# Mixer stage of a hybrid attention step on Trainium2: the order of VectorE's queue, three kinds of steps moved to GpSimd, and four buffers for the output weights

## What is computed

```
og  = rmsnorm(o_fwd + o_bwd, gla_norm) * silu(gg)            # gated linear attention, 8 heads of 64
s   = concat([q k_local * scale + mask, q k_context * scale, sink])
p   = softmax(s)[..., :-1]                                    # windowed attention, one sink logit per head
osw = p v
xs  = xs + g1 * (concat([og, osw]) @ w_o)
```

## Time and profile before

| | us |
|---|---|
| median of 3 runs (range) | 1693.15 (1691.63 to 1693.45) |
| the profiled execution, its own time | 1686.72 |
| its span | 1684.9 |
| slot 0 begins (first L1846) | 415.17 |
| slots 35, 46 begin | 605.74, 660.68 |
| the turn after the slots (L2187) | 699.05 |

### The profile page before, as it was taken

The page is one execution under the profiler, slowest core; times in us unless marked ns, Lnnn a source line. Parts: engine busy times, 40 slices in busy tenths (PEclk is TensorE's granted clock), DMA queues, the critical chain, the costliest instruction groups (busy, mean ns, idle before and its releaser), DMA issues. The chain is left out here.

```text
span 1684.9 us, 31914 instructions
## 1 busy us (share of the span) xinstructions
PE 1597.7 (95%) x11618; PEld 1396.7 (83%) x11618; DVE 1009.1 (60%) x1563; ACT 682.9 (41%) x1205; POOL 993.5 (59%) x738
## 2 busy tenths in 40 slices
PE   4999999998899987899999999999999999999997
PEld 1998778997778765688888999989978899998996
DVE  2733565666675565455876566665695545545468
ACT  2514224224454545312354444444535444444441
POOL 1711554655564865002487777777898667677672
PEclk7999999999999989999999999999999999999999
DMA  9354665659555554233662322313235132231322
GB/s 325 98 157 135 198 206 177 224 178 264 166 171 170 164 158 126 107 125 126 212 224 64 100 65 85 100 50 100 87 104 175 61 100 67 83 100 50 100 64 100
DMA packets 211450, 225.93 MB, mean 134 GB/s; under 512 B 52752, under 2 KB 171664, under 8 KB 208144
## 3 DMA queue, kind: packets, MB, share of 16 engines
q1 hardware_dynamic: 209248, 224.46, 41.8%
q10 hardware_dynamic: 2096, 0.02, 0.1%
HBM read 177.22 MB, written 47.24 MB: 133 GB/s over the span
## 5 line engine op out<-in xcount | busy, mean ns | idle before, releaser
L3127 PE MATMUL ff_banks<-h_xop,h_whi 128*128 128x320 f32 x888 | 275.2, 310 | 5.9 <-DVE wo_raw L2931 3.1
L3129 PE MATMUL ff_banks<-h_xop,h_whi 128*128 128x320 f32 x888 | 274.4, 309 | 0.0
L3128 PE MATMUL ff_banks<-h_xop,h_whi 128*128 128x320 f32 x888 | 274.3, 309 | 0.0
L2951 DVE TENSOR_TENSOR ff_acc<-ff_acc,ff_banks 128x512 f32<-128x512 f32 x294 | 199.3, 681 | 99.0 <-PE ff_banks L3156 98.9
L3154 PE MATMUL ff_banks<-h_wlo 128*128 128x512 f32 x600 | 234.3, 390 | 1.6 <-DVE ff_acc L2951 0.7
L3156 PE MATMUL ff_banks<-h_wlo 128*128 128x512 f32 x600 | 233.4, 389 | 0.0
L2793 POOL TENSOR_TENSOR h_whi<-mid_raw,h_whi 128x512 fp32r<-128x512 f32 x149 | 207.3, 1407 | 1.4 <-ACT h_whi L2645 1.4
L2805 POOL TENSOR_TENSOR h_wlo<-mid_raw,h_wlo 128x320 fp32r<-128x320 f32 x128 | 116.6, 912 | 129.4 <-ACT mid_raw L2682 129.4
L3127 PEld LDWEIGHTS ff_banks<-h_xop,h_whi 128*128 128x128 f32 x888 | 166.7, 188 | 9.5 <-issue 5.3
L3128 PEld LDWEIGHTS ff_banks<-h_xop,h_whi 128*128 128x128 f32 x888 | 166.7, 188 | 1.1
L3129 PEld LDWEIGHTS ff_banks<-h_xop,h_whi 128*128 128x128 f32 x888 | 166.7, 188 | 0.0
(11 more groups left out here) (306 smaller groups left out, 3757.9 us busy)
## 6 DMA issues: line engine op xcount, KB each, us to landing
mid_raw<-in_w_ff SPq DMA_DIRECT2D x124, 512.0 KB, 4.4
mid_raw<-in_w_ada SPq DMA_DIRECT2D x18, 1024.0 KB, 7.3
early_room<-qk_by_channel SPq DMA_DIRECT2D x20, 512.0 KB, 4.1
proj<-prj_stage SPq DMA_DIRECT2D x60, 152.0 KB, 1.9
mid_raw<-in_w_in SPq DMA_DIRECT2D x6, 1216.0 KB, 7.1
early_room<-in_w_ada SPq DMA_DIRECT2D x6, 1024.0 KB, 11.0
decays<-early_room SPq DMA_DIRECT2D x8, 640.0 KB, 4.5
early_room<-decays SPq DMA_DIRECT2D x20, 256.0 KB, 3.0
```

The source lines that it names most:

```text
L2951: dve.tensor_tensor(acc[:, p, at], acc[:, p, at], down[n % RING], ALU.add).then_inc(added, 1)
L3127: pe.matmul(out, w_hi[:, k], x_hi[:, k], start=(k == 0), stop=False)
L3128: pe.matmul(out, w_hi[:, k], x_lo[:, k], start=False, stop=False)
L3129: mm = pe.matmul(out, w_lo[:, k], x_hi[:, k], start=False, stop=(k == KH - 1))
```

## The change

It edits only the mixer.

- VectorE: the scaling of the output rows, the sink's exponent and the low parts of `w_o` leave its queue. In a slot the order is now: first part of the maxima, `finish`, second part, recurrence, `low_queries` of this slot's queries (before: at the start of the next slot), and the norm's sum of squares last and one slot later.
- GpSimd: it gets these steps. `sink_gap` writes `8*sink - peak` (the factor 1/8 is now in ACT's exponential), `mixed` scales the output rows, `wo.pool` subtracts. The gate product `si` is taken out of `pool_scale` into `pool_silu`, two slots after the sum; the rest of `pool_scale` comes two slots later than before.
- ACT: the square of a tile stands one slot later.
- Buffers: four for the raw pieces of `w_o` (loaded four slots ahead), two for `si`, two for `inv`. The loads of a linear-attention tile wait for `o` and `si` of the tile two before instead of its output, and are issued three slots ahead; its store comes two slots later.
- The tables of slots: `glo_at` and `wo_at` have other numbers.

```
+    def pool_silu(self, pool, n):
+        j = n % 2
+        pool.wait_ge(self.factor_ready, n + 1)
+        if n >= 2:
+            pool.wait_ge(self.out_ready, n - 1)
+        pool.tensor_tensor(self.si[:, j], self.gg[:, j], self.factor[:, j], ALU.mult).then_inc(self.si_ready, 1)
+
     def pool_scale(self, pool, n):
         j = n % 2
-        pool.wait_ge(self.factor_ready, n + 1)
-        if n:
-            pool.wait_ge(self.out_ready, n)
-        pool.tensor_tensor(self.si[:, :], self.gg[:, j], self.factor[:, j], ALU.mult).then_inc(self.si_ready, 1)
...
-    def dve(self, dve, n):
-        dve.wait_ge(self.whi_ready, n + 1)
-        dve.tensor_tensor(self.wlo[:, :, self.columns(n)], self.raw[:, n % 2], hi_view(self.whi)[:, :, self.columns(n)], ALU.subtract).then_inc(self.wlo_ready, 1)
+    def pool(self, pool, n):
+        pool.wait_ge(self.whi_ready, n + 1)
+        pool.tensor_tensor(self.wlo[:, :, self.columns(n)], self.raw[n % len(self.raw)], hi_view(self.whi)[:, :, self.columns(n)], ALU.subtract).then_inc(self.wlo_ready, 1)
...
-        glo_at = dict(zip((5, 8, 24, 27, 30, 33, 36, 39, 42, 46), range(NT)))
-        wo_at = dict(zip((37, 38, 40, 41, 44, 45, 48, 50), range(D // P)))
+        glo_at = dict(zip((5, 8, 24, 26, 29, 32, 35, 38, 41, 44), range(NT)))
+        wo_at = dict(zip((37, 38, 41, 42, 45, 46, 49, 50), range(D // P)))
...
+                def sink_gap(u):
+                    heads = slice(u % KV * HG, (u % KV + 1) * HG)
+                    pool.wait_ge(peak_ready, u + 1)
+                    if u >= QRING:
+                        pool.wait_ge(sout_ready, u - QRING + 1)
+                    pool.tensor_tensor(sb_in[:, u % QRING], sink8[:, heads], peak[:, u % 2, PK].bitcast(F32), ALU.subtract).then_inc(sin_ready, 1)
+
+                def mixed(u):
...
+                    pool.wait_ge(inv_ready, u + 1)
...
+                    pool.tensor_tensor(mixa[:, j, at:at + HG * DH].rearrange("p (h d) -> p h d", d=DH), out[:, :, 0:DH],
+                                       inv[:, u % 2].unsqueeze(2).broadcast_to([P, HG, DH]), ALU.mult).then_inc(o_ready, 1)
...
+                    if w in finish_at:
+                        mixed(finish_at[w])
+                    if w - 2 in glo_at:
+                        glo.pool_silu(pool, glo_at[w - 2])
                     if w in glo_at:
                         glo.pool_sum(pool, glo_at[w])
-                    if w - 2 in glo_at:
-                        glo.pool_scale(pool, glo_at[w - 2])
+                    if w - 4 in glo_at:
+                        glo.pool_scale(pool, glo_at[w - 4])
+                    for side in range(2):
+                        if loc_at.get((w, side), (0, 0))[1]:
+                            sink_gap(loc_at[w, side][0])
+                    if w - 1 in wo_at:
+                        wo.pool(pool, wo_at[w - 1])
...
-                        glo.act_square(act, glo_at[w - 1])
+                    if w - 2 in glo_at:
+                        glo.act_square(act, glo_at[w - 2])
...
-                    if w - 2 in glo_at:
-                        glo.dve(dve, glo_at[w - 2])
-                    if w - 1 in query_at:
-                        low_queries(query_at[w - 1])
                     ahead((w, 0))
-                    ahead((w, 1))
                     if w in finish_at:
                         finish(finish_at[w])
+                    ahead((w, 1))
                     if w in scores_at:
                         rec.dve_scores(dve, scores_at[w])
                     if w in outputs_at:
                         rec.dve_new(dve, outputs_at[w])
-                    if w in wo_at:
-                        wo.dve(dve, wo_at[w])
+                    if w in query_at:
+                        low_queries(query_at[w])
+                    if w - 3 in glo_at:
+                        glo.dve(dve, glo_at[w - 3])
```

More of the change, by code:

```diff
@@ L1123, in __init__ @@
         self.raw = room
-        self.w_in = [s.sem(f"wo_in{j}") for j in range(2)]
+        self.w_in = [s.sem(f"wo_in{j}") for j in range(len(room))]
         self.whi_ready, self.wlo_ready = s.sem("wo_hi_ready"), s.sem("wo_lo_ready")
@@ L1131, in sp_load @@
     def sp_load(self, sp, n):
[L1132 to L1134 removed]
+        if n >= len(self.raw):
+            sp.wait_ge(self.wlo_ready, n - len(self.raw) + 1)
+        sp.dma_start(self.raw[n % len(self.raw)], self.view[:, :, self.columns(n)]).then_inc(self.w_in[n % len(self.raw)], 16)
     def act(self, act, n):
[L1137 to L1138 removed]
+        act.wait_ge(self.w_in[n % len(self.raw)], 16 * (n // len(self.raw)) + 16)
+        act.activation(self.whi[:, :, self.columns(n)], self.raw[n % len(self.raw)], ACT.Copy).then_inc(self.whi_ready, 1)
     def done(self, eng):
@@ L1532, in mixer @@
         junk = s.sb("junk", [P, 3 * P])
-        topc, topl, den, inv = (s.sb(n, [P, HG]) for n in ("topc", "topl", "den", "inv"))
+        topc, topl, den = (s.sb(n, [P, HG]) for n in ("topc", "topl", "den"))
+        inv = s.sb("inv", [P, 2, HG])
         sb_in = s.sb("sb_in", [P, QRING, HG])
@@ L1551, in mixer @@
                         arena[:, 8 * GW:9 * GW])
-        wo = OutputWeights(s, a, whi, wlo, wo_raw)
+        wo_more = s.sb("wo_more", [P, 2, KD, P])
+        wo = OutputWeights(s, a, whi, wlo, [wo_raw[:, 0], wo_raw[:, 1], wo_more[:, 0], wo_more[:, 1]])
         mT = rec.ps[:, 1:3].rearrange("p b (k n) -> p (b k) n", n=P)
@@ L1744, in _ @@
             def _(pool):
+                def sink_gap(u):
[5 more added lines that the diff above has]
+                def mixed(u):
+                    n, kv = u // KV, u % KV
+                    j = n % 2
+                    out = sums[:, u % 2].rearrange("p (h d) -> p h d", d=DH + 1)
+                    pool.wait_ge(inv_ready, u + 1)
+                    if n >= 2 and kv == 0:
+                        pool.wait_ge(stored[j], 16 * (n // 2))
+                    at = kv * HG * DH
+                    pool.tensor_tensor(mixa[:, j, at:at + HG * DH].rearrange("p (h d) -> p h d", d=DH), out[:, :, 0:DH],
+                                       inv[:, u % 2].unsqueeze(2).broadcast_to([P, HG, DH]), ALU.mult).then_inc(o_ready, 1)
                 pool.memset(maskr[:, 1, :], 0.0).then_inc(filled, 1)
@@ L1766, in _ @@
                 rec.pool_scaled(pool, FIRST + 1)
+                sink_gap(0)
                 glo.pool_gain(pool)
-                for w in range(SLOTS):
+                for w in range(SLOTS + 2):
                     if w - 1 in outputs_at:
```

41 lines of the change are left out of this document (15 added, 26 removed).

## The result

The changed kernel takes a median of **1653.03 us** (1650.35 to 1653.57, 4 runs) against 1692.39 us (1687.46 to 1693.45) for the kernel before in the same comparison: a ratio of 0.977, 95% interval 0.9748 to 0.9792. That is 39 us less, where the forecast was 21, and it lies 3 us outside the range of 1656 to 1689. The profiled execution took 1652.52 us (span 1650.7), 34.2 us less than that of before.

A forecast was written before the change was run, and what follows sets the result against it. It took the PE as the bound, losing mixer time to waits for VectorE, with GpSimd next. Slots 35 to 57 gave 19, slots 0 to 34 gave 5, less 3 for the lock: 21 us off, 1672, range 1656 to 1689.

The forecast's parts named there:

- What bounds it, and the VectorE part: Mixer slots 35 to 57: PE waits 19.4 us for VectorE, held by less urgent steps; at most 29.6 us can return.
- GpSimd as the next bound in slots 35 to 45: GpSimd's 40 us queue up to the last tile's sum limits the gain there to 14.2 us of 23 possible.
- slot 46 begins about 40 + 3.6 - 2.9 = 40.7 us after slot 35: GpSimd's queue of 40 us, plus 3.6 late at slot 35, less 2.9 for about a slot of allowed lateness; before, 54.9.
- waits of the square of 2 to 6 us at slots 43 and 46: Sign the forecast is right: ACT's square waits for GpSimd's sum at slots 43 and 46, 2 to 6 us each.
- The first rival: Mixer: GpSimd doesn't bind, ACT and PE run ahead, nothing waits; 38 us come back, 1655; chance 0.14.
- Slots 46 to 57: GpSimd has 25 us left for 32 and doesn't bind; floor 32.0 against 38.4, 5 of the 6.4 us kept.
- Slots 0 to 34: Of some 12 us of PE waits for VectorE, 4 come back, plus 1 of clock behind slot 7: 5 us.
- The lock: Slots 35 to 45: VectorE's maxima held by GpSimd on the SBUF port, perhaps 0.6 us longer each; 3 us charged.
- The third rival: Mixer: GpSimd's steps near their longest through port conflicts, slot 46 begins 6 to 7 us later than before; 1700, chance 0.10.
- the reason given against this rival: The VectorE steps that stretched GpSimd's steps (scaling, subtraction) are the ones that leave VectorE.
- The base: Whole kernel: 21 us off the profiled 1686.7 gives 1665.7; the median of runs, 6.4 above it, gives 1672.
- No gain elsewhere: Outside the mixer, such as the MLP, the same times were expected, only shifted.

The follow-up runs named there:

- b_order: Kernel before with only VectorE's queue reordered (maxima first, low queries in their own slot, norm's sum later, subtraction last), nothing moved to GpSimd: 1679.33 us, ratio 0.9925.
- b_wo_pool: Kernel before with only the eight subtractions of w_o moved from VectorE to GpSimd, one slot later: 1678.01 us, ratio 0.9930.
- a_double: Changed kernel with each of the eight w_o subtractions issued twice on GpSimd: 1674.55 us, ratio 0.9919 to before.
- a_moves_back: Changed kernel with all three moves to GpSimd undone; order, later norm steps, tables and buffers stay: 1672.56 us, ratio 0.9902 to before.
- a_small_back: Changed kernel with the output rows' scaling and the sink's exponent back on VectorE, subtractions still on GpSimd: 1665.87 us, ratio 0.9866 to before.
- a_gate_double: Changed kernel with each of the ten gate products issued twice on GpSimd: 1662.06 us, ratio 0.9831 to before.
- a_norm_front: Changed kernel with the norm's sum of squares back at the head of VectorE's slot, still in its later slot: 1652.11 us, ratio 0.9785 to before.
- a_wo_back: Changed kernel with the eight w_o subtractions back on VectorE, last in their slot: 1659.27 us, ratio 0.9819 to before.

## Why the prediction was wrong, point by point

The direction and the places were right. Wrong were the step that makes GpSimd the bound of slots 35 to 45, the size of slots 0 to 34, the charge for the lock, and the base.

**What bounds it, and the VectorE part: right.** The low queries' waits went from 11.4 to 0.4 us, the spread's with them, and b_order and b_wo_pool show that the steps in front were the cause: each takes 10.6 to 10.8 us out alone. The clock in slots 35 to 45 came back to 1.00 with the waits. One term was too small: 2.88 us is not what every slot takes without a wait. The PE is busy for 33.05 us in these eleven slots at a clock of 1.00, more than the 31.7 counted.

**GpSimd as the next bound in slots 35 to 45: wrong for these slots.** The step that failed is "slot 46 begins about 40 + 3.6 - 2.9 = 40.7 us after slot 35"; it began after 36.33, and the gain was 18.6, not 14.2. Two of its three terms were too large. The queue up to the last sum took 38.07 us (597.35 to 635.42) and not 40, although all durations were as priced: only a step that needs its predecessor's result leaves a gap (0.07 to 0.13 us in the timeline), an independent one leaves none. GpSimd began that queue 1.9 us late, not 3.6. But the tie between the sum and the start of slot 46 doesn't hold at all. Slot 46 began 3.6 us before the sum was done in the change and 11.5 us before it in a_double: there the sum's end moved by 9.4 us and the slot's start by 1.5. With a_double's sum the formula would give 49.3 - 2.9 = 46.4 us; slot 46 began after 37.8. So 3.6 is where slot 46 happened to begin, not how early it can. What set the time of slots 35 to 45 is the PE itself, busy for 33.05 of 36.33 us, with 3.1 us of waits for ACT's copies and VectorE's maxima; ACT and VectorE didn't wait for GpSimd there. Slot 45, the longest with 4.14 us, takes the same in a_moves_back, where GpSimd has none of the moved steps.

What a late sum does hold is the work behind ACT's square. I had looked for waits of the square of 2 to 6 us at slots 43 and 46; there was one, of 1.6. Slot 46 lost nothing by it; slots 47 and 48 take 3.20 and 3.19 us where they take 2.88 and 2.53 in a_small_back, so 1.0 us is the most that it cost there. Made longer, the queue costs nearly its length (a_double, a_gate_double). So GpSimd is full and just in time. The first rival's time (1655, "GpSimd doesn't bind") came out, and for slots 35 to 45 its mechanism too; what it left out is that no room is left.

**Slots 46 to 57: right in size** (5 forecast, 5.25 measured), in part by luck. GpSimd was busy for 29.2 us there, not 25, and slot 55 takes 3.94 us where it took 2.51, in a part in which nothing was to change.

**Slots 0 to 34: 5 forecast, 9.4 measured** (10.9 without slots 0 and 1, which scatter). I had said that I take back 4 of 12 us of waits and named as reasons the sum of squares at the head and the sink's exponent. a_norm_front puts the first at nothing. What I had left out is the scaling of the output rows, behind the maxima of its slot and in front of the next ones; with the exponent it is worth 5.9 us alone and 6.4 in the change, and how the two share this is open. I had also put the later norm steps at nothing: another 5.4 came with them or, behind slot 28, with their table, 3.0 of it in slot 7. With b_order's 2.5 against them that is 9.3 of the 10.9; the rest is of the size of the scatter in slots 4 and 5.

**The lock: 3 charged, and it was right to name it but not to charge it in full.** The maximum of the peaks and the sum of the denominators did get longer. Groups of VectorE in the mixer, after; the first answers to the last row:

```profile
L2094 DVE TENSOR_TENSOR mix_peak<-mix_topl,mix_sink 128x4 fp32r<-128x4 f32 x19 | 9.4, 493 | 0.7
```

```profile
L2058 DVE TENSOR_TENSOR mix_peak<-mix_topl,mix_sink 128x4 fp32r<-128x4 f32 x19 | 6.8, 356 | 0.7
```

The mean of the peaks went from 356 to 493 ns, 2.6 us in all, where 0.6 us for each was the forecast's example. The PE's waits for the peaks are 2.8 us, against 1.4 before. But 18.7 us of exponents and scalings on VectorE are gone. The net was a gain: it is part of the small moves' 10.3 us.

**The third rival (GpSimd at its longest, 1700): did not come.** Single lines of GpSimd, in the change and in a_wo_back, where the subtractions are on VectorE; the first answers to the first row:

```profile
L1088 POOL TENSOR_TENSOR mix_glo_o<-mid_raw x10: 1270/1280/1289, 443.8 to 634.1; 128x512 f32<-128x512 f32 x10
```

```profile
L1088 POOL TENSOR_TENSOR mix_glo_o<-mid_raw x10: 1272/1285/2253, 449.7 to 636.8; 128x512 f32<-128x512 f32 x10
```

The longest sum went from 2.26 to 1.29 us with the change, and is back at 2.25 in a_wo_back. In b_order and a_moves_back, which have the subtractions on VectorE too, the sum stays at 1.30 and 1.29, and other 128x512 steps of GpSimd are the long ones: L1105 with 2.10, L1101 with 2.36 us. With the change no 128x512 step takes over 1.30, and in b_wo_pool and a_small_back, where of VectorE's moved steps only the subtractions are gone, none takes over 1.48. So the reason given against this rival holds, above all for the subtractions. The maxima and additions left on VectorE take 0.15 to 0.16 us at their shortest. By the rule of the Trainium skill ("SBUF — State Buffer", "Who interferes with whom") the first of the two keeps the port for its whole length; both rows and the pair in slot 38 (1.24 us, ending with GpSimd's product) agree.

**The base.** The sum was made against the profiled execution (1665.7) and moved up by 6.4 us to the median of before. The changed kernel's profiled execution and its median are 1652.5 and 1653.0: there was no such distance to carry. One set of seven executions of before lay 12 us apart (1684.7 to 1696.6), the other two 6 and 3 us, and four of the change 3 us. The base made 5.9 of the 19 us of the miss; 4.4 came from slots 35 to 45, 4.4 from slots 0 to 34, 3 from the lock, 0.3 from slots 46 to 57, about 1 from the mixer starting earlier. Why before scatters, and by how much more than the change, was not tried.

**No gain elsewhere: right.** From the turn to the end of the span, before took 1684.9 - 699.05 = 985.9 us and after 1650.7 - 664.92 = 985.8.

## What to carry to other kernels

In strictly ordered queues look for what stands in front of the step that the bounding engine waits for: a late long step is harmless at the end of a slot and costs its whole wait at the head, and a short one between two urgent steps costs in each slot. Edits that free the same engine don't add up one by one: here three alone gave 10.8, 10.6 and 6.4 us, and the change 34.8, because each alone uncovered the next wait (b_order and b_wo_pool show it; 5.4 us came with the later norm steps and their table). Before you price a newly loaded engine as a bound, name the step of the bounding engine that waits for it, and by which path. Here the forecast tied the start of a slot to the end of GpSimd's sum; a longer queue moved that end by 9.4 us and the start by 1.5, and the cost came up to two slots later, behind ACT's square.

## What the runs showed of the hardware

- A full GpSimd need not be slower: at 96% busy its 128x512 sums and gate products took 1.28 us with a longest of 1.29, and the 128x1024 subtraction 2.37 to 2.39. In the five traces with all subtractions on VectorE, before among them, its longest 128x512 step took 2.10 to 2.36.
- The price is on the other side. The denominators' 128x4 addition took 1.48 us beside a subtraction on GpSimd where it mostly takes 0.15 to 0.26. Timelines of VectorE and GpSimd in slot 55:

```profile
657.56 1.48 DVE L2109 TENSOR_TENSOR mix_den<-mix_sums,mix_sb_out 128x4 f32<-128x4 f32 x1
```

```profile
654.31 4.71 POOL L1151 TENSOR_TENSOR h_wlo<-mix_wo_more,h_whi 128x1024 fp32r<-128x1024 f32 x2
```

The two subtractions end at 659.02 and the addition at 659.04.

- The granted clock follows the waits down and up: 0.84 in slots 35 to 45 before, 0.96 in b_order, 0.89 in b_wo_pool, 1.00 after, 0.95 again with the gate products doubled. With a_gate_double slots 35 to 57 took 10.4 us more. The PE's waits for ACT rose from 2.2 to 6.8 us, and its busy time from 64.1 to 68.3 us for the same products, at the lower clock.
